# One fused stage for the first norm, the projections and both FoX attentions, with every cache page issued by SP

## The reference, cut to what matters

```python
def fox_attend(q, k, v, c_q, c_k, q_pos, k_pos):
    s = jnp.einsum('bqhd,bkhd->bhqk', q, k).astype(jnp.float32) * (DH_A ** -0.5)
    s = s + jnp.transpose(c_q, (0, 2, 1))[..., :, None] - jnp.transpose(c_k, (0, 2, 1))[..., None, :]
    s = jnp.where(k_pos[None, :] <= q_pos[:, None], s, -jnp.inf)
    p = jax.nn.softmax(s, axis=-1)
    return jnp.einsum('bhqk,bkhd->bqhd', p.astype(v.dtype), v)
...
    xn = rmsnorm(x, norm_mix)
    u = xn @ w_in
...
    logf = jax.nn.log_sigmoid((fl + b_f).astype(jnp.float32))
    if past is None:
        o_a = fox_prompt(q, k, v, logf)
    else:
        o_a = fox_sample(q, k, v, logf, *past)
```

## Time and profile before

| | us |
|---|---|
| median of 3 runs | 2316.41 (2313.51 to 2317.73) |
| profiled execution, first to last instruction (span) | 2311.8 |
| PE busy over the span | 1996.4 (86%) |
| DVE, ACT, POOL busy | 782.8, 394.1, 181.7 |
| DMA | 277.67 MB, mean 120 GB/s |
| first RWKV projection product starts at | 673.88 |

### The profile page before, as it was taken

One profiled execution on the slowest core, in us unless ns is written; L12 is line 12 of the kernel. 1 busy time (PEld: TensorE's weight loads), 2 busy tenths in 40 slices (PEclk: granted clock), 3 DMA queues, 4 the chain that ended last, 5 costly groups with the idle time before them and its releaser, 6 DMA issues. The chain is left out here.

```text
span 2311.8 us, 38704 instructions
## 1 busy us (share of the span) xinstructions
PE 1996.4 (86%) x15421; PEld 1352.3 (58%) x15421; DVE 782.8 (34%) x1567; ACT 394.1 (17%) x835; POOL 181.7 (8%) x358
## 2 busy tenths in 40 slices
PE   4999799967779997999999999789599659999990
PEld 3665477731238786676666666544345347777770
DVE  3000456621203656333333333259613401111115
ACT  4000133300002322111111111111001111111112
POOL 0000144300000000000000000000000231111110
PEclk9999689978899999999999999989699779999995
DMA  3110200069950000110101101172150068888836
GB/s 114 37 37 19 80 5 4 3 235 386 385 190 31 30 35 10 49 39 28 43 30 49 45 30 36 43 264 80 36 210 28 28 217 317 317 315 319 317 130 238
DMA packets 96512, 277.67 MB, mean 120 GB/s; under 512 B 22832, under 2 KB 31536, under 8 KB 86864
## 3 DMA queue, kind: packets, MB, share of 16 engines
q1 hardware_dynamic: 64704, 218.81, 26.3%
q10 hardware_dynamic: 18592, 34.61, 4.2%
q0 software_dynamic: 13072, 22.21, 3.0%
HBM read 244.30 MB, written 39.15 MB: 123 GB/s over the span
## 5 line engine op out<-in xcount | busy, mean ns | idle before, releaser
L1198 PE MATMUL gate_p<-rows,gate_w 128*128 128x352 f32 x768 | 284.1, 489 | 0.0
L952 PE MATMUL rw_pp<-rows,rw_w 128*128 128x264 f32 x896 | 205.8, 391 | 7.7 <-DMA rw_w<-in_w_in 7.7
L952 PEld LDWEIGHTS rw_pp<-rows,rw_w 128*128 128x128 f32 x896 | 171.5, 192 | 40.1 <-DMA rw_w<-in_w_in 7.9
L306 PE MATMUL fox_pp<-rows,fox_w 128*128 128x352 f32 x576 | 172.2, 462 | 4.2 <-DMA fox_w<-in_w_in 4.2
L1198 PEld LDWEIGHTS gate_p<-rows,gate_w 128*128 128x128 f32 x768 | 129.6, 190 | 53.5 <-issue 4.1
L306 PEld LDWEIGHTS fox_pp<-rows,fox_w 128*128 128x128 f32 x576 | 110.1, 191 | 66.1 <-DMA fox_w<-in_w_in 4.6
L1790 PE MATMUL x_p<-late 128*128 128x512 f32 (+1 forms) x288 | 128.5, 601 | 1.5 <-PEq L1513 1.5
L2081 PEld LDWEIGHTS moe_gu<-rows,wgu 128*128 128x128 f32 x1024 | 118.6, 194 | 9.0 <-issue 7.6
L2081 PEld LDWEIGHTS moe_gu<-rows,late 128*128 128x128 f32 x1024 | 116.9, 192 | 8.1 <-issue 8.1
L2081 PE MATMUL moe_gu<-rows,wgu 128*128 128x96 f32 x1024 | 118.4, 277 | 1.1 <-ACT rows L2104 1.1
L2081 PE MATMUL moe_gu<-rows,late 128*128 128x96 f32 x1024 | 116.5, 275 | 0.0
(11 more groups left out here) (357 smaller groups left out, 2906.6 us busy)
## 6 DMA issues: line engine op xcount, KB each, us to landing
wgu<-in_we_gu SPq DMA_DIRECT2D x16, 2048.0 KB, 7.9
late<-in_we_gu SPq DMA_DIRECT2D x16, 2048.0 KB, 8.0
wd<-in_we_down SPq DMA_DIRECT2D x16, 1024.0 KB, 11.8
late<-in_we_down SPq DMA_DIRECT2D x16, 1024.0 KB, 11.8
qkv<-in_cache_kT ACTq DMA_DIRECT2D x48, 256.0 KB, 6.2
qkv<-in_cache_kT SPq DMA_DIRECT2D x48, 256.0 KB, 6.4
qkv<-in_cache_v ACTq DMA_DIRECT2D x48, 256.0 KB, 9.0
qkv<-in_cache_v SPq DMA_DIRECT2D x48, 256.0 KB, 8.8
```

The costliest lines, as they stand in the source:

```text
L306: mm = pe.matmul(pp[j % 2][:, c, 0:N], w[:, j % 2, k, :], e.xnT[:, k, c * N:(c + 1) * N], start=(k == 0), stop=(k == KD - 1))
L952: mm = pe.matmul(pp[u % 2][:, c, 0:QN], w[:, n % 2, k, :], e.xnT[:, k, at:at + QN], start=(k == 0), stop=(k == KD - 1))
L1198: mm = pe.matmul(out[:, 0:GATE_N], gw[:, j % 2, k, :], e.xnT[:, k, at], start=(k == 0), stop=(k == KD - 1))
```

## The change

The five stages become one, stage_fox:

- x is also handed in turned (xT), so that no turning of x is needed. Four slices are loaded by SP and four by ACT; the constants are loaded by POOL. ACT squares each slice; ACT and DVE multiply it by the gain (xg). The first two projection tiles run on xg, and DVE multiplies their result by 1/rms (rb) afterwards; the other six run on e.xnT = xg x rb. Only q and k, eight tiles, are projected in this way. e.xnT is also stored to memory (xn_d).
- v is made as token rows directly, e.xnT being the weights and w_v streaming, 8 products of 512 columns for each of 9 token tiles. The gate's columns are made with the eight width slices in four column strips and summed by a second product.
- Prompt attention runs in 32 units of two heads and one query tile, in the order 7, 0, 6, 1, 5, 2, 4, 3 of tiles. The scores use 64 contraction rows, one head on each half of the array's rows. One DVE instruction per head (tensor_tensor_reduce) adds the gate sums of the keys and takes the minimum, in place of the extra rows and the maximum. Probabilities are normalised before they are turned, v's 64 columns are the weights and the turned probabilities stream, so that the output arrives turned.
- After the turns of each unit and ahead of its mix stands one of 34 slots of the cache attention: per group of four sequences 8 key slots (8 pages each, two per sequence), one slot without pages, 8 value slots. Two slots remain after the last unit.
- All 256 pages are issued by SP alone: 12 before the stores of k and v, 16 (places that lie over e.xnT) after the last v tile, the others as slots are used up. There are 28 places.
- The cache's logf is fetched by POOL with 128 indirect DMAs from a computed index.
- stage_rwkv_front loads e.xnT back from xn_d in four parts and waits for each before the products that use it.

```diff
+TILE_ORDER = (7, 0, 6, 1, 5, 2, 4, 3)
+PAGES_KEPT, PAGES_OVER_XN = 12, 16
+RING = PAGES_KEPT + PAGES_OVER_XN
+SLOT = 8
+BG = 4
+CHUNKS = NPG // 2
+SLOTS = [x for _g in range(NB // BG) for x in ([("keys", _g, _n) for _n in range(CHUNKS)] + [("first", _g, 0)]
+                                              + [("values", _g, _n) for _n in range(CHUNKS)])]
...
+        def entry(i):
+            x, r = divmod(i, SLOT)
+            g, y = divmod(x, 2 * CHUNKS)
+            b, j = (r // 2, r % 2) if y < CHUNKS else (r % BG, r // BG)
+            return (g * BG + b) * NPG + 2 * (y % CHUNKS) + j
...
+            for j in range(4, 2 * HP):
+                sp.wait_ge(made, j - 3)
+                sp.dma_start(w[:, j % 4], a["w_in"][j]).then_inc(w_loaded[j % 4], 16)
+                if j == 5:
+                    sp.wait_ge(xn_ready, KD)
+                    sp.dma_start(wv, a["w_v"]).then_inc(wv_loaded, 16)
+                    sp.dma_start(e.xn_d, e.xnT).then_inc(spilled, 16)
...
+            def load_page(i):
+                n = sp.value_load(table[0:1, entry(i):entry(i) + 1], min_val=0, max_val=a["cache_v"].shape[0] - 1)
+                if i >= RING:
+                    sp.wait_ge(pages_used, (i - RING) // SLOT + 1)
+                src = (a["cache_kT"][ds(n, 1)].squeeze(0) if is_key(i)
+                       else a["cache_v"][ds(n, 1)].rearrange("n p h d -> p (n h d)"))
+                sp.dma_start(place(i), src).then_inc(page_loaded[i // SLOT % SLOT], 16)
...
+            for i in range(PAGES_KEPT):
+                load_page(i)
...
+            sp.wait_ge(spilled, 16)
+            for i in range(PAGES_KEPT, RING):
+                load_page(i)
             sp.wait_ge(logf_kept, 1)
             sp.dma_start(a["logf_out"][0:SEQ, :].rearrange("(t p) h -> p t h", p=P), logf_tok[:, 0:TT, :]).then_inc(stored, 16)
             sp.dma_start(a["logf_out"][SEQ:NT, :], logf_tok[0:NS, TT, :]).then_inc(stored, 16)
-            sp.wait_ge(stored, 16 * (n + 6))
+            sp.wait_ge(stored, 16 * (NTT + 2))
+            for s in range(2):
+                sp.dma_start(ckb[:, 1, s], e.c_rows[2 + s:3 + s, :].to_broadcast([P, SEQ])).then_inc(ck_loaded[1], 16)
+            for i in range(RING, len(SLOTS) // 17 * 16 * SLOT):
+                load_page(i)
...
+            gates_of(0)
+            widen(0, 0)
+            widen(0, 1)
+            gates_of(1)
+            for x in range(len(SLOTS)):
+                kind, g, n = SLOTS[x]
+                if kind == "keys" and n + 2 < CHUNKS:
+                    widen(g, n + 2)
+                if kind == "values" and g == 0 and n in (0, 1):
+                    widen(1, n)
...
+            for k0 in (0, 4):
+                for c in range(3):
+                    for q in range(4):
+                        mm = pe.matmul(fa[32 * q:32 * q + 32, c, 0:N3], wf[:, k0 + q, :], e.xnT[:, k0 + q, c * N3:(c + 1) * N3],
+                                       start=(k0 == 0), stop=(k0 == 4))
...
+                    mm = pe.matmul((fa[0:n, 3], fb[0:n, 3])[t % 2], e.xnT[:, k, t * P:t * P + n], wv[:, k, :],
                                    start=(k == 0), stop=(k == KD - 1))
...
+                for c in range(0, n, 512):
+                    m = min(512, n - c)
+                    for s in range(2):
+                        pe.matmul(score[s][:, c:c + m], qk[half(s), p, t * P:(t + 1) * P], qk[half(s), HP + p, c:c + m],
+                                  start=True, stop=c + m < n)
+                for s in range(2):
+                    pe.matmul(score[s][:, t * P:n], e.identb[:], e.causalb[:], start=False, stop=True).then_inc(scored, 1)
...
+                        mm = pe.matmul(op[half(s)], v_tok[:, k, (2 * p + s) * DH:(2 * p + s + 1) * DH], probT[:, s, k, :],
+                                       start=(k == 0), stop=(k == t))
...
+                pe.wait_ge(page_loaded[x % SLOT], 16 * SLOT * (x // SLOT + 1))
+                for p in range(HP):
+                    for b in range(BG):
+                        mm = pe.matmul(dec[32 * b:32 * b + 32, 0:2 * P].rearrange("q (j n) -> q j n", j=2),
+                                       qs[:, g * BG + b, p, :], pair(x * SLOT + 2 * b)[:, :, p * P:(p + 1) * P],
+                                       start=(p == 0), stop=(p == HP - 1))
+                mm.then_inc(pages_used, 1)
...
+            scores(0)
+            for u in range(NU):
+                turn_probs(u, 0)
+                if u + 1 < NU:
+                    scores(u + 1)
+                turn_probs(u, 1)
+                slot(u)
+                mix(u)
...
+                dve.tensor_tensor_reduce(prob[:, u % 2, s, 0:n], score[s][:, 0:n], ckb[:, p % 2, s, 0:n], -0.125, 3.0e38,
+                                         ALU.add, ALU.min, stat[:, u % 2, s, 0:1]).then_inc(biased, 1)
...
+            for u in range(NU):
+                keep_high(u, 0)
+                if u + 1 < NU:
+                    bias(u + 1, 0)
+                keep_high(u, 1)
+                if u + 1 < NU:
+                    bias(u + 1, 1)
+                slot(u)
+                if u + 1 < NU:
+                    normalise(u + 1, 0)
+                    normalise(u + 1, 1)
...
+            sp.dma_start(w[:, 0], a["w_in"][8 + ORDER[0]]).then_inc(w_loaded[0], 16)
+            for b in range(4):
+                sp.dma_start(e.xnT[:, 2 * b:2 * b + 2], e.xn_d[:, 2 * b:2 * b + 2]).then_inc(xn_back[b], 16)
+            sp.dma_start(w[:, 1], a["w_in"][8 + ORDER[1]]).then_inc(w_loaded[1], 16)
...
-STAGES = [stage_norm, stage_fox_project, stage_fox_prepare, stage_fox_prompt, stage_fox_sample,
-          stage_rwkv_front, stage_rwkv_scan,
+STAGES = [stage_fox, stage_rwkv_front, stage_rwkv_scan,
```

More of the change, by code:

```diff
@@ L94, in shape_constants @@
     out["own_past"] = np.concatenate([np.where(o, 0.0, NEG) for o in own], 1).astype(np.float32)
[L96 to L103, removed]
+    out["gather8"] = (np.arange(P)[:, None] % NS == np.arange(H)[None, :]).astype(np.float32)
+    out["spread"] = (np.arange(P)[:, None] == np.arange(NS)[None, :] // TS).astype(np.float32)
     out["before"] = (i < j).astype(np.float32)
@@ new lines, in _ @@
+            pe.wait_ge(w_loaded[0], 16)
+            project(0, xg, range(KD)).then_inc(made, 1)
+            pe.wait_ge(sq_added, KD)
+            pe.wait_ge(ones_set, 1)
+            for t in range(NTT):
+                mm = pe.matmul(fa[0:size(t), 1, 500 + t:501 + t], acc[:, t * P:t * P + size(t)], e.ones[:, 0:1],
+                               start=True, stop=True)
+            mm.then_inc(sums_made, 1)
+            pe.wait_ge(w_loaded[1], 16)
+            project(1, xg, range(4))
+            pe.wait_ge(spread_set, 1)
@@ new lines, in slot @@
+            def slot(x):
+                kind, g, n = SLOTS[x]
+                if kind == "keys":
+                    keys(g, n)
+                elif kind == "first":
+                    turn_sample(g, 0)
+                else:
+                    values(g, n)
+            scores(0)
[6 more added lines that the diff above has]
+                mix(u)
@@ L391, in _ @@
+            for x in range(NU, len(SLOTS)):
+                slot(x)
+            turn_out(1, 0)
+            turn_out(1, 1)
         @block.scalar
         def _(act):
+            for k in range(1, KD, 2):
+                act.dma_start(xg[:, k], a["xT"][k]).then_inc(x_loaded[k], 16)
+            act.wait_ge(vec_loaded, 16)
+            for k in range(KD):
+                act.wait_ge(x_loaded[k], 16)
+                if k >= 3:
+                    act.wait_ge(sq_added, k - 1)
+                act.activation(sq[:, k % 2] if k else acc, xg[:, k], ACT.Square).then_inc(squared, 1)
+                if k % 2 == 0:
+                    act.wait_ge(squared, k + 1)
+                    act.activation(xg[:, k], xg[:, k], ACT.Copy, scale=e.v("norm_mix")[:, k:k + 1]).then_inc(xg_even, 1)
@@ new lines, in values, with slot @@
+            def values(g, n):
+                keep_sample(g, n + 1)
+                if n == CHUNKS - 1:
+                    st.then(dve, dve.reciprocal(stat_d[:, 11:12], stat_d[:, 10:11]))
+                    dve.wait_ge(d_mixed, g + 1)
+                    dve.tensor_scalar(o_sb, dec, stat_d[:, 11:12], None, ALU.mult).then_inc(d_out, 1)
+            def slot(x):
+                kind, g, n = SLOTS[x]
+                if kind == "keys":
+                    keys(g, n)
+                elif kind == "first":
+                    keep_sample(g, 0)
+                else:
+                    values(g, n)
@@ L878, in stage_rwkv_front @@
+            for x in range(NU, len(SLOTS)):
+                slot(x)
+            keep_out(1, 0)
+            keep_out(1, 1)
 def stage_rwkv_front(e):
     nc, a, sem = e.nc, e.a, e.sem
-    e.fox_mem.close()
     e.obT = e.sb("obT", [P, HP, NT])
```

1090 lines of the change are left out of this document (529 added, 561 removed).

## The result

The changed kernel took 2240.7 us in the median of four executions (2231.1 to 2245.1), the kernel before 2316.3 in the same comparison: ratio 0.967, 95% interval 0.9636 to 0.9698. That is faster, but by 76 us where I had forecast 167, and outside the range of 2090 to 2205. Six of the 38 executions of the kernel before that ran beside the experiments took 35 to 120 us more than its usual 2317, at a mean granted clock of 0.874 to 0.914 instead of about 0.93; the ratios leave such executions out.

The account below looks back on a forecast made before the run. SP's page issue, 1.12 us per page, was taken to bound the attention, not the rings. RWKV starting at 507 instead of 673.9 us saves 166.9, giving 2149.5 us; own range 2125 to 2175, with rivals' milder ends 2090 to 2205.

Parts of the forecast that it names:

- part 4: Cache gates on GpSimd: 128 indirect fetches at 1.28 us end at 177 us, 44 us to spare, cost nil.
- Rival C: Gate fetches: slot 1 waits for all 128, delaying later pages; slower above 3.1 us per fetch, 2368 at 3.5; chance 0.03.
- The figure of the Trainium skill: Gate fetches: a GpSimd-issued DMA stretched from about 620 to 3100 ns beside a VectorE copy, giving the time of before.
- Rival B: Attention loop is the bound: 2220 us if PE falls to 1.2 GHz, 2182 if upper bounds meet; chance 0.25.
- Part 1: Front (norm, projections, v, gate): first product at 13 us, PE ends at 208.9 us.
- Part 2: Cache pages: SP's issue at 1.12 us per page is the limit; last page issued at 488, stage ends at 497.
- the sentence of the Trainium skill: Page issue: several issuing engines save only initiation time, usually small beside transfer; by it pages would flow at 0.68 us.
- Part 3: Loop of 32 units and 34 slots keeps up: 6.2 us per unit against 8.96 per slot, so prompt attention costs nothing.
- The open term, two heads abreast: Loop's scores and mix on PE: 1.96 us each serial or 0.98 with both 64-row heads abreast; lower value taken.
- next late is PE: Attention loop: if pages came faster and its cover went, prompt attention on PE would be the bound.
- rival A: Pages not bound by SP, so loop-bound: RWKV at 437 us, 2079 us, or 2098 with slower loop; chance 0.12.
- Part 5: Start of RWKV projections: reloading normalised x takes 5.6 us, first product 503.8, plus 3.2 of later waits gives 507.

Follow-up runs that it names:

- e8_again: The changed kernel measured again, not one instruction altered: 2149.8 us, ratio 0.927 to the kernel before.
- e5: Changed kernel, indirect gate fetches kept, odd pages from the 29th on issued by GpSimd instead of SP: 2082.9 us, ratio 0.899 to the kernel before.
- e7: Changed kernel with cache gates by direct DMAs and half of the pages issued by GpSimd: 2084.4 us, ratio 0.900 to the kernel before.
- e17: e7 unaltered, measured again in the fifth group (direct fetches, half of the pages on GpSimd): 2083.0 us, ratio 0.899 to the kernel before.
- e16: e5 unaltered, measured again in the fifth group (indirect fetches, half of the pages on GpSimd): 2182.4 us, ratio 0.943 to the kernel before.
- e13: The changed kernel measured once more, unaltered, in the fourth group: 2250.9 us, ratio 0.971 to the kernel before.
- e15: Changed kernel with the second sequence group's 64 gate fetches moved from the front into the slot loop: 2256.4 us, ratio 0.972 to the kernel before.

## Why the prediction was wrong, and where it was right

**The step that failed is part 4**: "the cost is nil". It priced the 128 indirect fetches by their own duration and due time, and both were nearly right: they ended at 194 (I had 177; (192.9 - 14.7)/127 = 1.40 us apiece against 1.28), and the widening that slot 1 needs was not late. What the step did not price is what they do to the others. On some chips a dense row of them holds up the instructions of PE, SP, DVE and ACT over long stretches until it ends: 91 to 101 us in the changed kernel (2240.7 to 2250.9 against 2149.8). I had taken for the whole price of a fetch, but that row could not show the rest: where it stands, PE has little to do. A window of the kernel before around that row:

```profile
1820.00:1860.00 40.00, 7.99 (x37) 7.08 (x36) 16.90 (x75) 4.16 (x7) 17.86 (x19) 0.54 0.05 14
```

Rival C had the fetches as the danger, but by another way (slow fetches, slot 1 waits). They were at most 2.1 us each, and only GpSimd's own first widening waited for one, 1.3 us. The figure of the Trainium skill that I set beside C ("SBUF — State Buffer", section "A bandwidth-pool intuition that's wrong (but worth ruling out)", 3100 ns) was not seen. A DVE pass beside it did stretch a fetch, though: in e8_again the ones of 2.03 us (at 47.3, 49.7 and 54.9) lie beside DVE passes of 1.25 us, where the median is 1.0. Rival B's 2220 lies near the first measurement by accident: the loop was not the bound (PE waited for pages there), and the 91.5 us were lost ahead of it.

**All else adds up.** Where the stall is absent, on the very same kernel, the time is 2149.8 (e8_again) against 2149.5. Part of that is luck: the profiled span is 2148.6 against my 2144.9, and what lies around a span is 1.7 us and not 4.6. By steps, in the trace of e8_again:

- Part 1, front. First product at 17.4, not 13: x landed at 13.6, not 9.5. Here is what answers to the earlier trace rows:

```profile
13.63 1.28 ACT L692 ACT_TABLE_LOAD   x1 [13.63 <-DMA fox_work<-in_xT]
14.92 1.08 ACT L692 ACTIVATE v_tok<-fox_work 128x1056 f32<-128x1056 f32 x1
```

From the first product to the sixteen pages 212.6 - 17.4 = 195.2; my terms sum to 208.9 - 13 = 195.9, and 0.6 more to the pages.
- Part 2, pages. Sixteen in 17.35 us (18 forecast), 5.3 to the next burst (5), then 228 pages from 235.26 to 489.68: 254.4 us, 1.116 each (255.4 and 1.12). The last was issued at 489.7, forecast 488; the last copy ended at 500.3, forecast 497. That SP's issue is the limit, and not the rings, is shown by e5 and e7: a second issuer takes 2151.5 to 2084.4 with direct fetches, and 2149.8 to 2082.9 with indirect ones (each pair across the first two groups, neither of them hit). In the loop of e8_again (235 to 495 us) PE waited for pages 22 times, 55.6 us in all. On the sentence of the Trainium skill that I had set against this ("DMA: Bandwidth & Descriptors", section "Issuing engines are not separate DMA queues"): the time of initiation was not small beside the transfer here, and saving it was worth 67 us.
- Part 3, the loop keeps up. The open term, two heads abreast, came out at the lower value: scores and mix, in the changed kernel, take half of what they did (81.4 and 82.1 us busy before; lines view, busy and mean ns):

```profile
L569 PE MATMUL fox_b<-fox_work,v_tok 128*64 128x128 f32 x576 | 41.7, 293 | 6.0 <-issue 3.0 <-DVE dec_probT L877 2.8
L531 PE MATMUL fox_a<-qk 64*128 64x512 f32 (+3 forms) x192 | 41.0, 533 | 0.0
```

The add-and-minimum on DVE has a mean of 754 ns; I had taken 0.76 between 758 and 1400. In e17, where pages come faster, PE is busy for 171 of 190 us of the loop and RWKV starts at 442.2: "next late is PE" (the waits view puts none of PE's idle time there on a page, though the rings' share is 0.90), and rival A's price (437, 2079) is what a loop without SP's limit on pages really costs (442, 2083).

```profile
230.00:420.00 190.00, 171.47 (x1793) 100.83 (x1795) 114.62 (x345) 87.61 (x209) 69.44 (x120) 0.96 0.90 322
```

- Part 5. From SP's first load (500.5) to the first RWKV product 6.4 us; the 5.6 I had for it came from two weight tiles (1.05 MB), where 1.6 MB had to land. It starts at 506.9; I had 503.8, and 507 with all of the waits. Of these 3.2 a wait of 0.9 is seen at 516. From the first RWKV product to the end it is 2148.6 - 506.9 = 1641.7, before 2311.8 - 673.9 = 1637.9: 3.8 more, of which the rest is not traced.

**What stays open.** Why some chips stall and others don't: in three groups, and in the first measurement too, every execution with dense indirect fetches was hit; in the other two groups none is known to have been. That it is the chip, and not another thing that stays the same through a group, no run separates. Nor is it shown what the held instructions wait for; the view finds no semaphore for PE and SP and no releaser for DVE and ACT. In the hit profiles of the changed kernel there are stretches at full speed beside the fetches, for which I have no cause: from 17 to about 50 us in all, and up to 89 us in e16; later ones lie elsewhere in each (109 to 131 us in the first measurement, 118 to 133 in e13). Finally, every execution timed here was also recorded by the profiler, so no run says whether the stall exists without it.

## What to carry to other kernels

Price an instruction that moves to another engine by what it does to its neighbours, and ask of each row you price from whether those neighbours were busy where it was taken; if not, the price is a lower bound. A long, dense row of GpSimd's indirect DMAs beside dense TensorE work is best replaced by direct ones, where a register can hold the address, or spread out; on a chip that stalls this gave back 99 us of 2250. Where many transfers of 256 KB go by addresses from a table, count the issuing time: here 1.12 us per page on one queue against 0.68 on the rings, and a second issuer gave 67 us. The best version here, direct fetches and half of the pages on GpSimd, took 2083.0 to 2084.4 us on both kinds of chip, 10% less than the kernel before.

## What the runs showed of the hardware that I had not expected

- In the worst stretch of every hit profile (from about 140 us on in the changed kernel), most products followed each other by 1.4, 2.1 or 2.8 us, which are 2, 3 and 4 times 0.70 us; so do the starts of the first products that run faster again (229.06, 230.46, 233.26). It looks as if instructions were let through at a beat of 0.70 us. SP was held as well: 2.9 us per page instead of 1.09 in the front, 3.5 in the loop of e15. That DVE and ACT were held too, for 31.7 us behind a finished tile, stands with the result.
- Full speed comes back 3 to 10 us behind the start of the last fetch: 195.8 behind 192.9, 108.8 behind 100.0, 233.3 behind 223.2.
- Four executions that agree within 0.6% are no proof that a time is the kernel's own: the unaltered kernel had medians of 2240.7, 2149.8, 2248.4 and 2250.9 us in four measurements, while the medians of the kernel before stayed between 2316.2 and 2318.7 in the same comparisons.
